# RWKV rounds: the doubling series of a 64x64 nilpotent matrix rewritten as three steps with its fourth power

## The reference, cut to what matters

```python
def step(S, inp):
    r_t, w_t, k_t, v_t, a_t, b_t = inp
    sa = jnp.einsum('bhvk,bhk->bhv', S, a_t)
    S = S * w_t[:, :, None, :] + sa[..., None] * b_t[:, :, None, :] + v_t[..., None] * k_t[:, :, None, :]
    return S, jnp.einsum('bhvk,bhk->bhv', S, r_t)
```

## Time and profile before

| what | us |
|---|---|
| median of 3 runs | 2280.94 (2275.43 to 2285.91) |
| profiled execution, its own time | 2290.82 |
| its span, first to last instruction | 2289.0 |
| TensorE busy | 1965.0 (86%) |
| TensorE weight loads busy | 1367.0 (60%) |
| VectorE busy | 913.5 (40%) |
| ScalarE busy | 679.8 (30%) |
| GpSimd busy | 330.6 (14%) |

### The profile page before, as it was taken

How to read it: one execution, slowest core, us unless ns; L and a number is a source line. 1 busy time by engine, 2 the same in 40 slices (tenths; PEclk the granted TensorE clock), 3 DMA queues, 4 the chain that set the end, 5 groups by cost and what they waited for, 6 DMA issues and landing times. The chain is left out here.

```text
span 2289.0 us, 53938 instructions
## 1 busy us (share of the span) xinstructions
PE 1965.0 (86%) x23829; PEld 1367.0 (60%) x23829; DVE 913.5 (40%) x1635; ACT 679.8 (30%) x1491; POOL 330.6 (14%) x218
## 2 busy tenths in 40 slices
PE   6999999997979888998668799698999877977775
PEld 3777765444854444555344488688888865634443
DVE  3193325586032111111244468556767544111102
ACT  3233534575231000110032443544554212000001
POOL 1433310001411000000100145231123000000000
PEclk8999999799989988998888999799999987978888
DMA  8554442303355698778830031000000046899975
GB/s 294 188 216 147 166 165 105 116 0 111 111 190 218 221 346 325 268 265 314 314 106 28 1 111 56 11 4 3 4 4 4 4 128 230 303 382 355 370 287 183
DMA packets 133311, 380.85 MB, mean 166 GB/s; under 512 B 14394, under 2 KB 43670, under 8 KB 115926
## 3 DMA queue, kind: packets, MB, share of 16 engines
q1 hardware_dynamic: 114528, 343.82, 40.9%
q10 hardware_dynamic: 15094, 20.99, 3.1%
q0 software_dynamic: 3456, 12.58, 1.5%
HBM read 634.54 MB, written 25.95 MB: 289 GB/s over the span
## 5 line engine op out<-in xcount | busy, mean ns | idle before, releaser
L371 PE MATMUL banks<-parts 128*128 128x512 f32 (+1 forms) x1096 | 244.0, 374 | 14.5 <-POOL parts L1523 7.6
L1814 PE MATMUL banks<-arena 128*32 128x256 f32 x1696 | 220.5, 406 | 38.6 <-DMA arena<-in_exp_w_up_dram 38.6
L371 PEld LDWEIGHTS banks<-parts 128*128 128x128 f32 x1096 | 194.1, 191 | 55.0 <-POOL parts L2388 9.4
L1815 PE MATMUL banks<-arena 128*32 128x256 f32 x1696 | 220.4, 405 | 0.0
L1880 ACT ACTIVATE arena<-banks 64x256 f32<-64x256 f32 x78 | 29.7, 381 | 551.6 <-PE banks L1815 377.1
L1814 PEld LDWEIGHTS banks<-arena 128*32 128x32 f32 x1696 | 102.8, 116 | 119.4 <-DMA arena<-in_exp_w_up_dram 41.9
L371 PE MATMUL banks<-arena,ring 128*128 128x256 f32 (+1 forms) x528 | 158.4, 462 | 12.8 <-PEq L318 12.8
L379 DVE TENSOR_TENSOR arena<-banks,arena 64x256 f32<-64x256 f32 (+3 forms) x136 | 71.0, 522 | 231.8 <-ACT arena L1880 147.2
L2005 DVE COPY arena<-banks 128x256 f32<-128x256 f32 x78 | 33.2, 425 | 313.2 <-DMA y_sorted<-arena 233.7
L1836 PE MATMUL banks<-arena 128*32 128x256 f32 x1696 | 118.2, 426 | 37.5 <-DVE arena L1995 20.4
L371 PEld LDWEIGHTS banks<-arena,ring 128*128 128x128 f32 x528 | 104.5, 200 | 62.6 <-issue 51.3
(11 more groups left out here) (373 smaller groups left out, 3675.6 us busy)
## 6 DMA issues: line engine op xcount, KB each, us to landing
arena<-in_exp_w_gate_dram SPq DMA_DIRECT2D x106, 1024.0 KB
arena<-in_exp_w_up_dram SPq DMA_DIRECT2D x106, 1024.0 KB
arena<-in_exp_w_down_dram SPq DMA_DIRECT2D x53, 2048.0 KB
ring<-in_exp_w_gate_dram SPq DMA_DIRECT2D x50, 1024.0 KB
ring<-in_exp_w_up_dram SPq DMA_DIRECT2D x50, 1024.0 KB
ring<-in_exp_w_down_dram SPq DMA_DIRECT2D x25, 2048.0 KB
ring<-in_w_mod_dram SPq DMA_DIRECT2D x24, 2048.0 KB, 9.2
ring<-in_ab_w_in_dram SPq DMA_DIRECT2D x10, 2048.0 KB, 14.1
```

The costliest lines, as they stand in the source:

```text
L371: m = nc.tensor.matmul(o, a, b, start=first and n == 0, stop=last and n == len(pairs) - 1)
L1814: nc.tensor.matmul(o[r:r + BLOCK, 0:256], x, up[:, k, c], start=k == 0, stop=k == KD - 1)
L1815: m = nc.tensor.matmul(o[64 + r:64 + r + BLOCK, 0:256], x, gate[:, k, c], start=k == 0, stop=k == KD - 1)
```

## The change

The pair product "D4 T2" becomes a single product T2 of 64 columns, and D4 is no longer computed; D4t is still computed from D2 and D2t. D8t is gone as well. In place of T4 = T2 + D4 T2 and T8 = T4 + D8 T4 stand H1 = T2 + D4 T2, H2 = T2 + D4 H1 and T8 = T2 + D4 H2, all with D4t as first operand. H1 and H2 lie in the tiles of D2 and D2t. ScalarE no longer copies D4 and D8t; VectorE adds H1 and H2 where it added T4.

```diff
-                s.update(D4=s["D"], D4t=s["Dt"], D8t=s["D2t"], N=s["D"], V1=s["D2"], V2=s["D2t"], V3=s["Dt"], U=s["D2t"])
-                s["T D2"] = beside("D2", "T")
+                s.update(D4t=s["Dt"], H1=s["D2"], H2=s["D2t"], N=s["D"], V1=s["D2"], V2=s["D2t"], V3=s["Dt"], U=s["D2t"])
@@ pe_round
-                    take_pair("D4 T2", "D4", "T2")
+                    take("T2")
                     for g in range(2):
-                        ready(g, "T1", "D2", "D2t")
-                        each("D4 T2", [("D2t", "T D2")], g, parts=("D4", "T2"))
+                        ready(g, "T1", "D2t")
+                        each("T2", [("D2t", "T")], g)
                     take("D4t")
                     for g in range(2):
+                        ready(g, "D2")
                         each("D4t", [("D2", "D2t")], g)
...
-                    take("T4")
+                    take("H1")
                     for g in range(2):
                         ready(g, "T2", "D4t")
-                        each("T4", [("D4t", "T")], g)
-                    take("D8t")
+                        each("H1", [("D4t", "T")], g)
+                    take("H2")
                     for g in range(2):
-                        ready(g, "D4")
-                        each("D8t", [("D4", "D4t")], g)
+                        ready(g, "H1")
+                        each("H2", [("D4t", "H1")], g)
...
                     take("T8")
                     for g in range(2):
-                        ready(g, "T4", "D8t")
-                        each("T8", [("D8t", "T")], g)
+                        ready(g, "H2")
+                        each("T8", [("D4t", "H2")], g)
@@ act_round
                     for g in range(2):
-                        act.wait_ge(*at_(("T2 read", g)))
-                        copied("D4", g)
-                    for g in range(2):
                         copied("D4t", g)
...
-                    for n_ in ("D8t", "N", "V1"):
+                    for n_ in ("N", "V1"):
@@ dve_round
-                    for g in range(2):
-                        add_power("T4", g)
+                    for n_ in ("H1", "H2"):
+                        for g in range(2):
+                            s = now[g]
+                            dve.wait_ge(*at_((n_ + " product", g)))
+                            go(vadd(s[n_], s["T"], view(g, n_)), g, n_, n_ + " read")
```

## The result

| | median us | runs |
|---|---|---|
| before | 2283.41 (2275.43 to 2291.32) | 20 |
| changed | 2295.23 (2281.85 to 2299.98) | 20 |

The ratio is 1.0044 (95% interval 1.0032 to 1.0055): slower by 10 us, between 7 and 13. The forecast was 2281, range 2273 to 2290; the time lies outside it, and the change is a real one, though just inside the 0.5% that I had called no change.

A forecast was written before the change was run, and what follows sets the result against it. VectorE's queue (second T4 addition plus a fixed 3.68 us tail), not TensorE, was taken to set N. 4 x 0.34 + 3 x 0.09 - 1.48 = +0.15 us, applied to the 2280.94 median, gave 2281 us, range 2273 to 2290.

The forecast's parts named there:

- TensorE's saving: From T2's start to the second H1 product: 6.55 us instead of 8.21 in round 4, 1.66 us earlier.
- The passes H1 to H2 to T8: Product, addition, product in a chain: second-group products 2.00 us apart, between 1.87 and 2.04.
- N against the start of the pair: N's start counted from D4 T2's start: 0.34 us later in rounds 1 to 4, 0.09 later in 5 to 7.
- Round 8: Last round, without the four products for the next chunk: TensorE's saving counts there, -1.48 us.
- The sum: All rounds' shifts together: +0.15 us, with other passes from -0.9 to +0.5.
- Copies, banks, ScalarE, GpSimd at no cost: Between T2 and N: D4t's copies in time, bank turns covered, ScalarE's saved copies off the path, GpSimd shifting with N.
- rival (b): TensorE's longer idle time before N drops the clock after each N: 7 x 5.6 = 39 us, 2320; chance 0.03.
- the idle time of 2.5 us: TensorE's wait before N in rounds 1 to 4, instead of 0.69; about 2.2 in 5 to 7.
- the evidence against it: Against a clock fall: idle times of 0.96 and 1.75 us within 5 us had left the clock at 1.00.
- (a): TensorE is the bound after all and its saved time is won: 12.4 us, 2268.5; chance 0.06.
- (c): An unseen wait, such as TensorE's instruction supply ("issue"), takes up to 14 us more, 2295; chance 0.05.

The follow-up runs named there:

- delay2: Kernel before with two more VectorE products that change nothing behind the T4 additions in rounds 1 to 7; 2294.4 us, ratio 1.0052.
- delay3: Kernel before with three more VectorE products that change nothing behind the T4 additions in rounds 1 to 7; 2302.4 us, ratio 1.0075.
- before_a_late: Kernel before with the two VectorE products for the next a moved behind the T8 additions; 2278.3 us, ratio 0.9984.
- delay1: Kernel before with one more VectorE product that changes nothing behind the T4 additions in rounds 1 to 7; 2287.3 us, ratio 1.0019.
- wide: Changed kernel with T2's product 128 columns wide again, the half that was D4 left unread; 2301.4 us, ratio 1.0083.
- y_late: Changed kernel with the products for the next a and also Y1's additions moved behind the T8 additions; 2265.2 us, ratio 0.9925.
- a_late: Changed kernel with the two VectorE products for the next a moved behind the T8 additions; 2273.5 us, ratio 0.9954.
- before_y_late: Kernel before with the products for the next a and also Y1's additions moved behind the T8 additions; 2284.5 us, ratio 1.0010.
- fill: Changed kernel with useless TensorE products into N's bank ahead of N in rounds 1 to 7; 2281.8 us, ratio 0.9986.

## Why the prediction was wrong

Point by point, with what was measured in its place:

- TensorE's saving: D4 and T2 as two products of 64 columns. From T2's start to the second H1 product 6.58 us (1616.94 to 1623.52), forecast 6.55. Right.
- The passes H1 to H2 to T8: 2.01 and 2.01, forecast 2.00. Right.
- N against the start of the pair: 1631.12 - 1616.94 = 14.18 us in round 4, 13.80 before: +0.38, forecast +0.34; in round 5 15.62 against 15.51: +0.11, forecast +0.09. Round 8: 14.06 against 15.30: -1.24, forecast -1.48. The sum is +0.6 us, forecast +0.15. Right within half a microsecond, and with it the claim on which it rests, that TensorE's time comes back as idle time before N.
- Copies, banks, ScalarE, GpSimd at no cost: nothing of theirs shows between T2 and N, apart from the waits forecast. Right.
- **The step that failed is the clock: the sum has no term for it, and rival (b), which would have been that term, was priced wrongly and given 0.03.** Its place and its cause were right, and so was the idle time of 2.5 us. Two things were wrong. The first is the price: from the long stretch at 0.50 in round 0 I took 5.6 us for a fall, 39 in all and 2320, which put it out of reach of the range. A fall here lasts 3.4 us and costs 1.55, so that six cost 9.3; with the +0.6 that makes 9.9 us, and the ratio says 10. That these two agree so well is in part luck: the pair of profiles shows 7.2 in the stage, and the second profile of the changed kernel 4.2 with five falls. The second is the evidence against it: two idle times of 0.96 and 1.75 us in a row at clock 1.00 were taken as more than one of 2.48. The changed kernel itself, delay2 and delay3 say otherwise.

Both could have been read from the trace of the kernel before. Outside the rounds it has 14 stretches at 0.50 that last 3.4 us each, and some of them follow an idle time of 2.0 us, if in thinner work than that of the rounds. One such place, TensorE's timeline and then the busy time by stretch up to it, in it and behind it (columns as above):
```profile
654.04 1.33 PE L442 MATMUL banks<-arena,ident 128*128 128x128 f32 x8 [2.00 <-DVE arena L436]
```
```profile
651.00:654.80 3.80, 1.18 (x14) 0.92 (x15) 0.95 (x1) 0.93 (x2) 0.31 (x1) 1.00 0.18 23
654.90:658.20 3.30, 3.30 (x19) 0.98 (x21) 2.72 (x6) 0.00 (x0) 0.00 (x0) 0.50 0.19 40
658.30:661.00 2.70, 2.70 (x26) 1.03 (x19) 2.63 (x7) 0.60 (x1) 0.00 (x0) 1.00 0.19 39
```
And the place taken as evidence against a fall goes on: 1.65 us more of idle time end at 1834.73, and 0.6 us into the next one, at 1835.9, the clock falls for 6.8 us:
```profile
1835.90:1842.70 6.80, 4.70 (x20) 2.87 (x21) 5.63 (x11) 4.32 (x10) 2.72 (x6) 0.50 0.66 212
```
A single idle time of about 2.0 us can go either way: at the start of round 4 TensorE waits 2.02 us for the new state without a fall in the kernel before, and at the same place the clock fell with 2.00 us in before_a_late (at 1601.1) and with 1.99 in delay1 (at 1598.1).

Rivals (a) and (c) did not occur; "issue" idle time between T2 and T8 is nil.

The Trainium skill, TensorE: Matmul & The Clock Gate, section Why this matters for your kernels, says to leave no idle gaps above a certain length between bursts of matmuls, or the array goes back to half rate; that length is greater than the longest idle time before N here, 2.86 us. This case's traces agree on the effect and not on the length: 11 of 14 idle times of 2.2 to 2.5 us in the changed kernel came with a fall to 0.50, and 3 of 14 in wide. The prediction names the rule without its length; taken with it, the rule would not have spoken against this change, and here the measurement decides.

What stays open: why the clock falls less often in wide at the same idle times, how many falls an execution that wasn't profiled has, and how much of y_late's lead over a_late is its own.

## What to carry to other kernels

Before cutting work from the busiest engine, find what releases it next; if another engine's queue does, the saving turns into idle time, and the first thing to change is that queue's order. And idle time of TensorE is not free: ahead of N, idle times of 0.4 to 1.4 us left the clock alone here, and most of those of 2.2 to 2.5 us in the changed kernel did not. Before giving such a rival its price and its chance, look in the whole trace of the kernel before for short stretches at 0.50 and for the idle time ahead of each: they show the length of a fall, which one long stretch after a cold start doesn't. A fall that may or may not happen widens the range by its count: here seven places x 1.55 us.

## What the runs showed of the hardware that I had not expected

- At N the clock fell at idle times of 2.0 to 2.9 us, but not at each: 6 and 5 of 7 in two profiles of one kernel, none of 14 at 0.7 to 1.4 us in delay1 and a_late. Elsewhere it fell near shorter ones: at 1716.7 in before_y_late, 0.8 us behind the end of 1.54 us, and at 1740.7 in fill, 0.6 us behind the end of 1.93 us. The fall at N began from 0.95 us before to 1.38 us after TensorE had gone back to work, so nearly all of the slow products are those behind the gap, which themselves wait for nothing.
- VectorE's products of two SBUF operands take 0.69 us alone (L2895 in the changed kernel, round 4) and 1.30 to 1.65 us while GpSimd works (L2904 in before_y_late, round 6), while its additions out of PSUM stay at 0.69. Moving the products for a behind T8 puts them beside GpSimd's part: in round 4 of a_late they take 1.54 and 1.41 us. Whether that gives back some of a_late's gain was not tested.
